# The S5 mixer of a hybrid decoder in chunks of four time steps, with its loads in another order

## The chip, the cores and the metric

The kernel runs on one core of a Trainium2 chip. The metric is device time in microseconds (us) of one execution, lower is better. Engines: TensorE (PE in the profile, its weight loads PEld), VectorE (DVE), ScalarE (ACT), GpSimd (POOL), and SyncE (SP), which here only issues DMAs.

## The reference, cut to what matters

Two decoder layers over 512 tokens of width 1024, in float32. Each has a mixer and then a mixture of 64 experts of which each token takes two. The change is in the mixer of layer 0. That mixer projects the normed tokens to 1536 columns: 512 for S5, 512 for the RG-LRU input, 512 for the RG-LRU gate.

```
def s5_mixer(u, ...):                       # u: 512 steps x 32 groups x 16 channels
    lb = exp((lam_re + i lam_im) dt)        # one complex decay per state, 64 states in a group
    bu[l] = Bbar u[l]                       # 16 channels -> 64 complex states, per group
    s[l]  = lb * s[l-1] + bu[l]             # over the 512 steps
    y = Re(C s) + D u
    y = gelu(y);  return y * sigmoid(y @ glu_w + glu_b)
def rglru_mixer(...): conv of width 4, two gates (sigmoid), h[l] = a[l] h[l-1] + b[l], times gelu(gate)
out = concat(ya, yb) @ w_out;  x = x + out
```

## The kernel before

Channels or states lie on the 128 partitions and time along the free axis. Two groups of 64 states fill the 128 partitions, so the 32 groups make NS5 = 16 blocks, each with a real and an imaginary part over T = 512 steps.

Four instruction streams run in order (even_tensor, even_vector, even_scalar, even_gpsimd) and meet by semaphores. SP's stream and POOL's hold the loads, in their order.

- Start: norm_sums, norm_rows, norm_tensor (32 transposes, L209) and the evacuations L186 (ACT) and L201 (DVE) make hT, the normed input with channels on partitions. even_tensor then projects in 12 blocks of 128 columns, 8 matmuls each (L309), evacuated by proj_out (ACT).
- Parameters: even_vector derives decays and Bbar in some sixty small operations, which go through the helpers tt, ts and stt (L484, L488, L490, L493): each waits for the one before.
- Tables: per block, phases (DVE) makes a phase for each of the 512 steps, table_scalar (ACT) four functions of it, tables (DVE) the cosine and sine. With these a complex decay becomes a rotation of the input, a real decay, and a rotation back.
- Scan: per block s, bu (PE, L345) makes the block's input from its 32 channels. products (DVE, L616 to L619) rotates it, L626 and L627 add, two scans of 512 steps (L636, L637) run with the real decay, GpSimd rotates back (L685 to L688), and PE contracts with C (L367: four matmuls of 32 output rows).
- RG-LRU: conv (L577, L579), gates (L332), exp/tanh/sqrt (L441 to L446), four scans (L600), ahead of the S5 scan on DVE.
- End: GELU (L454), GLU matmuls (L376), sigmoid (L457), product (L643), output projection in 8 tiles of 512 columns (out_lru L352 for the RG-LRU half, L387 for the S5 half), added to x (L406), and the norm of the next part.
- The experts: three slots of two experts each (ring buffers 0 to 3, wbuf, region_a) are filled by first_pair and moe_sync; slots 0 and 1 may be filled when the mixer has let go of their memory, slot 2 after the output projection. PE works through 32 pairs of experts (L1262, L1272, L1281, L1292).

A matmul in float32 shows as two MATMUL instructions in the profile, a transpose as one.

## Time and profile before

| | us |
|---|---|
| median of 3 runs (lowest, highest) | 1800.18 (1798.22, 1801.88) |
| the profiled execution's own time | 1798.09 |
| its span in the profile | 1796.2 |
| PE busy, of the span | 1405.1 (78%) |
| DVE busy | 577.4 (32%) |
| ACT busy | 305.9 (17%) |
| POOL busy | 384.0 (21%) |

The span holds, in order: the mixer of layer 0 (0 to 346 us), its experts (to about 900), the attention mixer of layer 1 (to about 1210) and its experts (to the end). Busy shares are means over all of these; the stage that is changed is the first, and the expert stages have the DMA engines full. A line given with a helper (L484) holds the work of many callers, told apart by shapes.

### The profile page before, as it was taken

What the parts mean: (1) busy time and instruction counts of PE and PEld (TensorE: products, weight loads), DVE (VectorE), ACT (ScalarE), POOL (GpSimd) and SP (SyncE); (2) the same over time, 40 slices, a digit from 0 to 9 for tenths busy, and PEclk for the clock granted to TensorE, in tenths of its full rate; (3) what the DMA queues carried; (4) which work ended last, traced back from release to release, by engine and by line L of the source; (5) the groups of instructions that cost most, each with busy time, mean ns of one, the idle gap of its engine ahead of it and who ended that gap; (6) DMA issues with size and microseconds to landing.
All of it is one profiled execution on the core that took longest, in us unless ns stands there. A gap on an engine that the chain in (4) does not pass through costs nothing.

```text
span 1796.2 us, 18735 instructions
## 1 busy us (share of the span) xinstructions
PE 1405.1 (78%) x5548; PEld 615.6 (34%) x5548; DVE 577.4 (32%) x1063; ACT 305.9 (17%) x594; POOL 384.0 (21%) x484
## 2 busy tenths in 40 slices
PE   5966879849878877777838969994897887887883
PEld 3421213523323323332325437544333322332331
DVE  5979991251111111111140665315111111111112
ACT  3671001101110001001023343211111001100100
POOL 2006881012322222222100000000222222222120
PEclk9986989969999999999968989996899989998997
DMA  7102003269999999999732020307699999999994
GB/s 215 47 8 86 1 0 152 95 253 391 390 403 403 406 400 399 407 411 389 309 105 100 0 106 1 153 35 281 255 396 400 395 402 398 402 412 396 393 366 179
DMA packets 81971, 464.27 MB, mean 258 GB/s; under 512 B 13504, under 2 KB 15584, under 8 KB 32384
## 3 DMA queue, kind: packets, MB, share of 16 engines
q1 hardware_dynamic: 68352, 435.81, 61.6%
q0 software_dynamic: 11840, 21.52, 3.8%
q10 hardware_dynamic: 1728, 6.29, 0.9%
q8 instruction: 29, 0.48, 0.1%
q14 instruction: 22, 0.18, 0.0%
HBM read 453.14 MB, written 18.94 MB: 263 GB/s over the span
## 4 chain that ended last, share of the span: by engine, by line
PE 37%; SPq 28%; DVE 18%; DMA 6%; issue 6%; ACT 3%; POOL 1%; POOLq 0%; DVEq 0%; ACTq 0%
SPq L1410 18%; PE ps L1272 12%; SPq L1415 10%; PE ps L1292 5%; DMA ring<-in_moe_w 3%; PE ps L398 3%; PE ps L1262 2%; PE ps L777 2%; DVE ring L637 2%; PE ps L387 2%; PE ps L209 1%; DMA region_a<-ytok 1%; PE ps L830 1%; DVE extra L484 1%; PE ps L352 1%
## 5 line engine op out<-in xcount | busy, mean ns | idle before, releaser
L1272 PE MATMUL ps<-ring,region_b 128*64 128x512 f32 x1408 | 347.7, 650 | 79.9 <-issue 53.1
L1376 DVE TENSOR_TENSOR extra<-extra,ps 128x256 f32<-128x256 f32 x64 | 27.0, 421 | 611.9 <-ACT extra L1328 611.9
L1272 PEld LDWEIGHTS ps<-ring,region_b 128*64 128x64 f32 x1408 | 116.9, 150 | 308.0 <-issue 269.8
L1272 PE MATMUL ps<-wbuf,region_b 128*64 128x512 f32 x320 | 159.5, 657 | 44.9 <-DMA region_a<-in_moe_w 28.0
L1292 PE MATMUL ps<-ring,extra 128*64 128x512 f32 x704 | 160.8, 598 | 34.8 <-DVE extra L1382 34.8
L1272 PE MATMUL ps<-region_a,region_b 128*64 128x512 f32 x320 | 159.7, 657 | 0.0
L1216 POOL DMA_INDIRECT region_b<-hrow,icol x128 | 118.6, 926 | 156.2 <-issue 156.2
L1228 POOL DMA_INDIRECT ytok<-extra,icol x128 | 112.2, 876 | 162.8 <-issue 162.8
L1328 ACT ACTIVATE extra<-ps 128x256 f32<-128x256 f32 x64 | 24.6, 384 | 589.0 <-PE ps L1272 589.0
L1389 DVE COPY extra<-ps 128x512 f32<-128x512 f32 x64 | 44.3, 692 | 248.0 <-PE ps L1292 248.0
L1226 POOL COPY icol<-blkidx 64x2 int32 (+1 forms) x64 | 11.2, 176 | 462.9 <-DVE extra L1389 462.9
L1272 PEld LDWEIGHTS ps<-wbuf,region_b 128*64 128x64 f32 x320 | 46.8, 151 | 152.1 <-issue 140.2
L1292 PEld LDWEIGHTS ps<-ring,extra 128*64 128x64 f32 x704 | 49.9, 136 | 115.4 <-issue 89.8
L1262 PE MATMUL ps<-con,region_b 128*128 128x128 f32 x512 | 75.7, 292 | 17.2 <-DMA region_b<-hrow,icol 17.2
L1262 PEld LDWEIGHTS ps<-con,region_b 128*128 128x128 f32 x512 | 63.2, 195 | 67.9 <-issue 67.9
L1292 PE MATMUL ps<-wbuf,extra 128*64 128x512 f32 x320 | 73.1, 597 | 16.7 <-DVE extra L1382 16.7
L1334 ACT ACTIVATE extra<-ps 128x512 f32<-128x512 f32 x64 | 38.2, 597 | 277.0 <-PE ps L1292 277.0
L309 PE MATMUL ps<-region_b,wbuf 128*128 128x512 f32 x192 | 83.1, 593 | 0.8 <-ACT region_b L186 0.8
L209 PE MATMUL ps<-con,region_a 128*128 128x128 f32 x128 | 24.1, 375 | 53.3 <-DVEq L161 35.6
L1214 POOL COPY icol<-blkidx 64x2 int32 (+1 forms) x64 | 13.6, 213 | 218.3 <-DVEq L1190 217.5
L1321 ACT ACTIVATE region_b<-ps 128x512 f32<-128x512 f32 x64 | 38.2, 597 | 93.9 <-PE ps L1262 93.9
L1371 DVE COPY region_b<-ps 128x512 f32<-128x512 f32 x64 | 44.3, 692 | 24.4 <-PE ps L1262 24.3
(288 smaller groups left out, 1746.6 us busy)
## 6 DMA issues: line engine op xcount, KB each, us to landing
ring<-in_moe_w SPq DMA_DIRECT2D x264, 1024.0 KB, 26.5
wbuf<-in_moe_w SPq DMA_DIRECT2D x80, 1024.0 KB, 26.4
region_a<-in_moe_w SPq DMA_DIRECT2D x40, 1024.0 KB, 28.7
region_a<-ytok SPq DMA_DIRECT2D x16, 512.0 KB, 4.6
wbuf<-in_ev_w_in SPq DMA_DIRECT2D x3, 2048.0 KB, 10.6
hrow<-region_a ACTq DMA_DIRECT2D x8, 512.0 KB, 15.3
wbuf<-in_mla_w_in SPq DMA_DIRECT2D x2, 1408.0 KB, 26.9
wbuf<-in_mla_w_uq SPq DMA_DIRECT2D x1, 2304.0 KB, 8.6
```

The lines of the kernel that those rows point to most:

```text
L209: last = TE.transpose(ps[:, 2 * c + k // 4, (k % 4) * P:(k % 4 + 1) * P], hs[:, k, :], ident)
L309: last = TE.matmul(ps[:, PB[n], :], w[:, k, (m % 4) * P:(m % 4 + 1) * P], hT[:, k, :], start=k == 0, stop=k == KC - 1)
L398: last = TE.matmul(ps[:, (n + 2) % 4, :], lhs(k, n // 2), wout[n % 2][:, k, :], start=k == 0, stop=k == KC - 1)
L1216: G.indirect_dma_start(xin[j][CAP * g:CAP * g + n, :], None, hrow[l], bass.IndirectOffsetOnAxis(ap=icol[0:n, 2 * j + g:2 * j + g + 1], axi ...
L1228: G.indirect_dma_start(ytok[l], bass.IndirectOffsetOnAxis(ap=icol[0:n, 4 + 2 * j + g:5 + 2 * j + g], axis=0), yo[j][CAP * g:CAP * g + n, : ...
L1262: last = TE.transpose(ps[:, k // 4, (k % 4) * PAIR:(k % 4 + 1) * PAIR], xin_block(j, k), ident)
L1272: last = TE.matmul(ps[CAP * g:CAP * (g + 1), 2 + j, :], xtr[j][:, k, CAP * g:CAP * (g + 1)], up_weights(2 * slot + g, k), start=k == 0, st ...
L1292: last = TE.matmul(ps[CAP * g:CAP * (g + 1), 6 + nh, :], hidT[j][:, f, CAP * g:CAP * (g + 1)], w2[2 * slot + g][:, f * D + nh * 512:f * D ...
L1371: V.tensor_copy(xtr[j][:, 0:4, :].rearrange("p k s -> p (k s)"), ps[:, 0, :])\
L1389: V.tensor_copy(yo[j][:, 0:512], ps[:, 6, :]).then_inc(ml["s_ye"][l], 1)
L1410: nc.sync.dma_start(w13[b][:, n, :], src).then_inc(s, 16)
L1415: nc.sync.dma_start(w2[b], src).then_inc(s, 16)
```

## The change

S5 works in chunks of LC = 4 steps, so NC = 128 chunks.

- The S5 projection is computed with time on the partitions (32 matmuls of 512 columns, one set for each step i within a chunk), evacuated by ACT to u4 and turned by 16 transposes to uT: for each block of 32 channels a tile of (4 steps x 32 channels) x 128 chunks.
- DVE makes the decay's powers 0 to 4 and with them bd, Bbar times the powers; 32 transposes and 8 evacuations make wb. GpSimd makes wc (C times the powers) and the decay tile dec.
- Input of a chunk: two matmuls of 128 columns for each block (32 in all) give it for all 128 chunks.
- Between chunks: one table of 16 x 128 phases, one rotation, and two scans over all 16 blocks side by side (2048 elements), with the fourth power of the decay; the first element of each block has decay zero.
- Within a chunk: a Toeplitz matrix of 128 x 128 for each block, made by 128 small matmuls (function toeplitz), evacuated by ACT (toep_out) and given D on its diagonal by GpSimd.
- Output: 64 matmuls with the Toeplitz tiles and 128 with the states before each chunk, all 128 rows deep, 32 output rows wide, 128 columns long, into four PSUM banks; GELU reads them there.
- The RG-LRU's vector part now stands behind the S5 scan. All of out_lru comes after the GLU matmuls.
- Loads: the identity ahead of x, the S5 columns of the input weights first; B and C as one transfer in place of six; both early expert slots when the S5 output and the RG-LRU are done, ahead of the barrier.
- The small parameter work up to the phase step moved ahead of the evacuations L186 and L201.

The removed code is in the functions printed above. Core of the diff:

```diff
 QK = NOPE + ROPE
...
+            TE.wait_ge(s_ev_x[0], 16)
+            hs = hT.rearrange("p k (c i) -> p k i c", i=LC)
+            for i in range(LC):
                 for k in range(KC):
-                    last = TE.matmul(ps[:, PB[n], :], w[:, k, (m % 4) * P:(m % 4 + 1) * P], hT[:, k, :],
+                    last = TE.matmul(ps[:, i, :], hs[:, k, i, :], wcol[0][:, k, :], start=k == 0, stop=k == KC - 1)
+                last.then_inc(s_s5p, 1)
...
+            TE.wait_ge(s_ev_x[1], 16)
+            project(wcol[1], 0, 4)
+            TE.wait_ge(s_s5e, U4E)
+            for q in range(MT):
+                for g in range(4):
+                    last = TE.transpose(ps[:, q, g * P:(g + 1) * P],
+                                        u4[:, 4 * q + g, :, :].rearrange("p i n -> p (i n)"), ident)
+                last.then_inc(s_s5p, 1)
+            for m in range(1, MT):
+                project(wcol[1], m, 4 + m)
...
+            for b in range(2):
+                for q in range(MT):
+                    if b:
+                        TE.wait_ge(s_s5e, U4E + q + 1)
+                    else:
+                        TE.wait_ge(s_pje, q + 1)
+                    for g in range(4):
+                        last = TE.transpose(ps[:, (4, 0)[b] + q, g * P:(g + 1) * P],
+                                            bd[b][:, 4 * q + g, :, :].rearrange("p i n -> p (i n)"), ident)
+                    last.then_inc(s_s5p, 1)
+
+            TE.wait_ge(s_s5e, WBE)
+            for hf in range(2):
+                for g in range(8):
+                    s = 8 * hf + g
+                    for b in range(2):
+                        last = TE.matmul(ps[:, (4, 0)[hf] + 2 * b + g // 4, (g % 4) * P:(g % 4 + 1) * P],
+                                         wb[b][:, s * P:(s + 1) * P], uT[:, s, :], start=True, stop=True)
+                last.then_inc(s_s5p, 1)
...
+            def toeplitz(q, bank):
+                for g in range(4):
+                    s = 4 * q + g
+                    for b in range(2):
+                        for i in range(LC):
+                            last = TE.matmul(ps[32 * i:32 * i + 32, bank, g * P + 32 * i:(g + 1) * P], b0[b][:, s, :],
+                                             wc[b][:, s, 0:LC - i, :].rearrange("p j n -> p (j n)"),
+                                             start=g == 0 and b == 0, stop=g == 3 and b == 1)
+                last.then_inc(s_s5p, 1)
+
+            TE.wait_ge(s_wc, 2)
+            TE.wait_ge(s_pre, 1)
+            toeplitz(0, 6)
+            toeplitz(1, 7)
...
+            TE.wait_ge(s_ev_x[2], 16)
+            TE.wait_ge(s_pre, 2)
+            project(wcol[0], 0, 0)
+            project(wcol[0], 1, 1)
+            TE.wait_ge(s_gts, 2 * MT)
+            toeplitz(2, 4)
+            toeplitz(3, 5)
+            project(wcol[0], 2, 2)
+            project(wcol[0], 3, 3)
...
+            TE.wait_ge(s_wc, 5)
+            for q in range(MT):
+                for j in range(LC):
+                    for g in range(4):
+                        r = slice(32 * g, 32 * g + 32)
+                        TE.matmul(ps[r, 4 + q, j * NC:(j + 1) * NC], toep[:, 4 * q + g, 32 * j:32 * j + 32],
+                                  uT[:, 4 * q + g, :], start=j == 0, stop=False)
+            for q in range(MT):
+                TE.wait_ge(s_st, q // 2 + 1)
+                for j in range(LC):
+                    for b, st in enumerate((pa, pc)):
+                        for g in range(4):
+                            r = slice(32 * g, 32 * g + 32)
+                            s = 4 * q + g
+                            last = TE.matmul(ps[r, 4 + q, j * NC:(j + 1) * NC], wc[b][:, s, j + 1, :],
+                                             st[:, s * NC:(s + 1) * NC], start=False,
+                                             stop=j == LC - 1 and b == 1)
                 last.then_inc(s_cy, 1)
...
+            TE.wait_ge(s_yb, MT)
+            TE.wait_ge(s_wb[0], 16)
+            TE.wait_ge(s_wb[1], 16)
+            for n in range(4):
+                out_lru(n)
...
+            lru_out(1)
+            S.wait_ge(s_ph, 1)
+            S.activation(tabs, ph, ACT.Sin, scale=math.pi).then_inc(s_sn, 1)
+            alink(S.activation(tk, ph, ACT.Abs))
+            S.activation(tk, tk, ACT.Sin, scale=-math.pi, bias=halfpi).then_inc(s_sn, 1)
+            S.wait_ge(s_sn, 1)
+            S.activation(tabc, tabs, ACT.Square).then_inc(s_sn, 1)
+            lru_out(2)
+            lru_out(3)
+            for n in range(2 * MT):
+                S.wait_ge(s_s5p, UTE + n + 1)
+                S.activation(wb[n // MT][:, (n % MT) * T:(n % MT + 1) * T], ps[:, ((4, 0)[n // MT] + n % MT), :],
+                             ACT.Copy).then_inc(s_s5e, 1)
+
+            S.wait_ge(s_wc, 3)
...
+            for dst, (p1, p2, op) in ((bd[0], (pwr, pwi, ALU.subtract)), (bd[1], (pwi, pwr, ALU.add))):
+                for i in range(LC):
+                    V.tensor_tensor(bt4[0][:, :, i, :], qr, up(p1, LC - 1 - i), ALU.mult)
+                    ins = V.tensor_tensor(bt4[1][:, :, i, :], qi_, up(p2, LC - 1 - i), ALU.mult)
+                vlink(ins)
                 for g in range(2):
                     r = slice(64 * g, 64 * g + 64)
-                    tt(dst[r, :, 16 * g:16 * g + 16], btmp[r, :, :], btmp2[r, :, :], op)
+                    tt(dst[r, :, :, 16 * g:16 * g + 16], bt4[0][r, :, :, :], bt4[1][r, :, :, :], op)
             V.nop().then_inc(s_brd, 1)
...
+            tt(by_group(ph), tcb, rho_hi[:, :, None].to_broadcast([P, NS5, NC]), ALU.mult)
+            ts(tk, ph, ROUND, ALU.add)
+            ts(tk, tk, -ROUND, ALU.add)
+            tt(ph, ph, tk, ALU.subtract)
+            tt(by_group(tk), tcb, rho_lo[:, :, None].to_broadcast([P, NS5, NC]), ALU.mult)
+            tt(ph, ph, tk, ALU.add)
+            V.nop().then_inc(s_ph, 1)
...
+            for hf in range(2):
+                cols = slice(hf * HC, (hf + 1) * HC)
+                bank = (4, 0)[hf]
+                V.wait_ge(s_s5p, XH + hf + 1)
+                ur = ps[:, bank:bank + 2, :].rearrange("p b n -> p (b n)")
+                ui = ps[:, bank + 2:bank + 4, :].rearrange("p b n -> p (b n)")
+                V.tensor_tensor(pa[:, cols], ur, tabc[:, cols], ALU.mult)
+                V.tensor_tensor(pb[:, cols], ui, tabs[:, cols], ALU.mult)
+                V.tensor_tensor(pc[:, cols], ui, tabc[:, cols], ALU.mult)
+                vlink(V.tensor_tensor(pd[:, cols], ur, tabs[:, cols], ALU.mult))
+                V.nop().then_inc(s_pre, 1)
+            V.tensor_tensor(pa, pa, pb, ALU.add)
+            tt(pc, pc, pd, ALU.subtract)
+            V.wait_ge(s_wc, 4)
+            V.tensor_tensor_scan(pb, dec, pa, 0.0, ALU.mult, ALU.add)
+            vlink(V.tensor_tensor_scan(pd, dec, pc, 0.0, ALU.mult, ALU.add))
+            V.memset(by_group(pa)[:, :, 0:1], 0.0)
...
+                cols = slice(hf * HC, (hf + 1) * HC)
...
+                vlink(V.tensor_tensor(part(pc, 1, NC), part(pb, 0, NC - 1), part(tabs, 0, NC - 1), ALU.mult))
+                vlink(V.tensor_tensor(pb[:, cols], pd[:, cols], tabs[:, cols], ALU.mult))
+                vlink(V.tensor_tensor(pd[:, cols], pd[:, cols], tabc[:, cols], ALU.mult))
+                V.tensor_tensor(part(pa, 1, NC), part(pa, 1, NC), part(pb, 0, NC - 1), ALU.subtract)
+                V.tensor_tensor(part(pc, 1, NC), part(pc, 1, NC), part(pd, 0, NC - 1), ALU.add).then_inc(s_st, 1)
 
...
+            G.wait_ge(s_prm, 2)
+            pwr, pwi = pw
...
+            G.tensor_tensor(t1, co(cre), up(pwr), ALU.mult)
+            glink(G.tensor_tensor(t2, co(cim), up(pwi), ALU.mult))
+            for g in range(2):
+                r = slice(64 * g, 64 * g + 64)
+                glink(G.tensor_tensor(wc[0][r, :, :, 16 * g:16 * g + 16], t1[r, :, :, :], t2[r, :, :, :], ALU.subtract))
+            glink(G.tensor_scalar(cre, cre, -1.0, None, ALU.mult))
+            G.tensor_tensor(t1, co(cre), up(pwi), ALU.mult)
+            glink(G.tensor_tensor(t2, co(cim), up(pwr), ALU.mult))
+            for g in range(2):
+                r = slice(64 * g, 64 * g + 64)
+                glink(G.tensor_tensor(wc[1][r, :, :, 16 * g:16 * g + 16], t1[r, :, :, :], t2[r, :, :, :], ALU.subtract))
+            G.nop().then_inc(s_wc, 1)
+            G.wait_ge(s_brd, 1)
+            G.tensor_copy(b0[0], bd[0][:, :, LC - 1, :])
+            glink(G.tensor_copy(b0[1], bd[1][:, :, LC - 1, :]))
...
+            sp.dma_start(con[:, 0:P], a["p_const"][:, 0:P]).then_inc(s_id, 16)
...
+            sp.dma_start(wcol[0], wv[:, :, 0:512]).then_inc(s_ev_x[0], 16)
+            sp.dma_start(con[:, P:C_END], a["p_const"][:, P:C_END]).then_inc(s_con, 16)
+            sp.dma_start(wcol[1], wv[:, :, 512:1024]).then_inc(s_ev_x[1], 16)
+            sp.wait_ge(s_s5p, LC)
             sp.dma_start(wcol[0], wv[:, :, 1024:1536]).then_inc(s_ev_x[2], 16)
...
+            sp.wait_ge(s_pj, 2 * MT)
+            sp.dma_start(glu, a["p_glu_w"]).then_inc(s_gw, 16)
+            sp.dma_start(wout0[1], wo[:, :, 512:1024]).then_inc(s_wb[1], 16)
+            sp.wait_ge(s_st, 1)
+            sp.dma_start(wout0[0], wo[:, :, 0:512]).then_inc(s_wb[0], 16)
+            sp.wait_ge(s_cy, MT)
+            sp.wait_ge(s_yb, MT)
             first_pair(0, 0)
-            sp.wait_ge(s_bar, 4)
             first_pair(0, 1)
```

## Rows read from the trace of the kernel before

**Rows 1.** Windows: each engine's busy us (xinstructions), granted PE clock, DMA share, GB/s.
```profile
380.00:400.00 20.00, 11.13 (x46) 5.76 (x48) 5.79 (x18) 1.88 (x2) 6.04 (x9) 0.55 0.39 156
400.00:420.00 20.00, 18.48 (x94) 7.39 (x92) 3.58 (x7) 2.56 (x5) 3.96 (x6) 1.00 0.81 331
440.00:460.00 20.00, 18.35 (x93) 8.01 (x91) 3.70 (x8) 2.69 (x6) 5.92 (x8) 1.00 1.02 384
860.00:880.00 20.00, 16.17 (x74) 6.58 (x70) 3.37 (x7) 2.56 (x5) 1.94 (x3) 0.91 0.91 353
```

**Rows 2.** Chain of waits in order of time: start, us, what.
```profile
294.11 6.87 PE ps L352 x16
342.21 0.70 DVE x L406
```

**Rows 3.** DVE in order of time, scan of S5: start, us, engine line operation tiles.
```profile
221.91 1.75 DVE L627 TENSOR_TENSOR ring<-ring 128x512 f32<-128x512 f32 x1
223.58 0.68 DVE L616 TENSOR_TENSOR extra<-ps,ring 128x512 f32<-128x512 f32 x1
225.97 1.21 DVE L636 TENSOR_TENSOR_SCAN ring<-smalls,ring 128x512 f32<-128x512 f32 x1
227.10 2.22 DVE L637 TENSOR_TENSOR_SCAN ring<-smalls,ring 128x512 f32<-128x512 f32 x1
229.83 1.75 DVE L627 TENSOR_TENSOR extra<-extra 128x512 f32<-128x512 f32 x1
```

**Rows 4.** POOL over the same stretch.
```profile
221.48 1.62 POOL L685 TENSOR_TENSOR region_a<-ring 128x512 f32<-128x512 f32 x1 [1.16 <-DVE ring L637]
223.07 1.72 POOL L686 TENSOR_TENSOR region_a<-ring 128x512 f32<-128x512 f32 x1
224.75 1.26 POOL L687 TENSOR_TENSOR region_a<-ring 128x512 f32<-128x512 f32 x1
225.98 2.26 POOL L688 TENSOR_TENSOR region_a<-ring 128x512 f32<-128x512 f32 x1
```

**Rows 5.** PE in order of time: start of the projections; GLU; last expert matmuls of a pair.
```profile
24.61 20.84 PE L309 MATMUL ps<-region_b,wbuf 128*128 128x512 f32 x48 [0.83 <-ACT region_b L186]
...
103.52 7.76 PE L332 MATMUL ps<-extra,region_a 64*64 64x512 f32 x24 [14.13 <-ACT ring L435]
...
280.11 14.00 PE L376 MATMUL ps<-region_a,extra 128*128 128x512 f32 x32 [2.28 <-ACT region_a L454]
...
408.30 7.04 PE L1272 MATMUL ps<-ring,region_b 128*64 128x512 f32 x32
```

**Rows 6.** PE in attention, tiles of 128 columns, in order of time.
```profile
1081.00 0.39 PE L828 MATMUL ps<-ring 128*128 128x128 f32 x2
1081.23 0.39 PE L829 MATMUL ps<-con 128*128 128x128 f32 x2
1081.54 0.48 PE L830 MATMUL ps<-ring 64*128 64x128 f32 x2
```

**Rows 7.** Groups of instructions, 0 to 330 us: shapes xcount, busy us, mean ns.
```profile
L209 PE MATMUL ps<-con,region_a 128*128 128x128 f32 x32 | 6.1, 376 | 17.7 <-DMA con<-in_p_const 17.7
L484 DVE TENSOR_TENSOR extra<-extra,smalls 128x256 f32<-128x256 f32 x4 | 1.7, 424 | 0.1
```

**Rows 8.** DVE and ACT in order of time: small operations, table load, Sin.
```profile
8.29 1.04 ACT L178 ACTIVATE extra<-x 128x1024 f32<-128x1024 f32 x1
36.51 1.65 DVE L484 TENSOR_TENSOR smalls<-smalls 128x16 f32<-128x16 f32 x8
122.47 1.28 ACT L465 ACT_TABLE_LOAD   x1
123.77 0.63 ACT L465 ACTIVATE region_a<-region_a 128x512 f32<-128x512 f32 x1
```

**Rows 9.** Windows of 2 us around an idle stretch of PE, columns as in rows 1.
```profile
92.00:94.00 2.00, 0.00 (x0) 0.00 (x0) 1.90 (x4) 0.39 (x1) 0.00 (x0) 1.00 0.00 0
94.00:96.00 2.00, 0.00 (x0) 0.00 (x0) 1.77 (x5) 1.94 (x4) 0.00 (x0) 0.57 0.00 0
```

More of the change, by code:

```diff
@@ L20 @@
 NS5 = 16
+LC = 4
+NC = T // LC
 H = 8
@@ L241, in hybrid_decoder @@
+        iT = r1[:, 2048:4096].rearrange("p (m t) -> p m t", m=MT)
+        gT = regb[:, 0:2048].rearrange("p (m t) -> p m t", m=MT)
+        glu = regb[:, 2048:4096].rearrange("p (k n) -> p k n", k=MT)
+        yg = pb.rearrange("p (m t) -> p m t", m=MT)
+        ya = pd.rearrange("p (m t) -> p m t", m=MT)
         s5p = small(16 * 3)
         lam_re, lam_im, ldt = s5p[:, 0:16], s5p[:, 16:32], s5p[:, 32:48]
-        s5q = [small(16) for _ in range(14)]
+        s5q = [small(16) for _ in range(15)]
@@ L244, in hybrid_decoder @@
+        pw = [small(16 * (LC + 1)).rearrange("p (s j) -> p s j", s=NS5) for _ in range(2)]
+        dskip = small(16)
+        eye32 = small(32)
         chp = small(MT * 10)
@@ L355, in even_tensor @@
-            bu(0)
-            bu(1)
-            bu(2)
-            TE.wait_ge(s_pje, 12)
-            for s in range(NS5):
-                if s + 3 < NS5:
-                    bu(s + 3)
-                TE.wait_ge(s_st, s + 1)
-                if s % 4 == 0 and s >= 8:
-                    TE.wait_ge(s_yd, s // 4 - 1)
-                r = slice(32 * (s % 4), 32 * (s % 4) + 32)
-                for j, (cm, g) in enumerate(zip((0, 2, 1, 1), prod[s % 2])):
-                    last = TE.matmul(ps[r, (s // 4) % 2, :], cmat[:, cm, s, :], g, start=j == 0, stop=j == 3)
+                    TE.matmul(ps[:, 4 + (n + 2) % 4, :], gT[:, k, (n // 2) * P:(n // 2 + 1) * P],
+                              wout0[n % 2][:, MT + k, :], start=k == 0, stop=False)
@@ L386, in even_tensor @@
                 for k in range(MT):
-                    last = TE.matmul(ps[:, (n + 2) % 4, :], uT[:, k, (n // 2) * P:(n // 2 + 1) * P],
-                                     wout[n % 2][:, k, :], start=False, stop=k == MT - 1)
+                    last = TE.matmul(ps[:, 4 + (n + 2) % 4, :], ya[:, k, (n // 2) * P:(n // 2 + 1) * P],
+                                     wout0[n % 2][:, k, :], start=False, stop=k == MT - 1)
                 last.then_inc(s_op, 1)
@@ L430, in even_scalar @@
-            proj_out(6)
-            proj_out(7)
+            S.activation(l1, l1, ACT.Ln, bias=1.0).then_inc(s_pra, 1)
+            for i in range(LC):
+                S.wait_ge(s_s5p, i + 1)
+                S.activation(u4[:, :, i, :], ps[:, i, :].rearrange("p (s n) -> p s n", s=NS5), ACT.Copy)\
+                    .then_inc(s_s5e, 1)
+            lru_out(0)
+            for q in range(MT):
+                S.wait_ge(s_s5p, U4E + q + 1)
+                S.activation(uT[:, 4 * q:4 * q + 4, :].rearrange("p s c -> p (s c)"), ps[:, q, :], ACT.Copy)\
+                    .then_inc(s_s5e, 1)
@@ L432, in even_scalar @@
+            S.wait_ge(s_wc, 3)
+            toep_out(0, 6)
+            toep_out(1, 7)
             for m in range(MT):
@@ L483, in tt, with lru_out @@
+        def lru_out(m):
+            S.wait_ge(s_pj, m + 1)
+            if m == 0:
+                S.wait_ge(s_xpad, 1)
+            S.activation(xT[:, m, 3:3 + T], ps[:, 4 + m, :], ACT.Copy).then_inc(s_pje, 1)
         def tt(o, p, q, op):
```

438 lines of the change are left out of this document (178 added, 260 removed).

## The prediction

> **What bounds the kernel now.** I read the windows first, to see which stages can carry a gain onward. From 400 to 880 us the DMA engines are full (share 0.81 to 1.02, 331 to 384 GB/s), and from 380 to 400 us they are at 0.39 [rows 1]: by then the three expert slots are full, and loading goes on when PE lets go of the first. So the experts of layer 0 end a fixed time after their first pair starts. That start hangs on the mixer's end by the same norm and routing in both kernels. Earlier expert loads gain nothing: the slots were full before PE used them.
>
> Next the chain of waits in order of time: the output projection ends when DVE adds its last tile at 342.2 us [rows 2]. Everything behind moves with this mark. Hence: new time = 1798.1 (the profiled execution's own time) minus the shift of 342.2. That execution lies 2.1 below the median of the runs, so I add 2.1.
>
> Then DVE and POOL in the scan, which the chain crosses from 142 to 268 us: DVE is never idle, a block takes 7.9 us (L627 starts at 221.91 and at 229.83), and 16 of them make 127 us [rows 3]. The same L627 that takes 1.75 us holds 0.6 us of work: it starts at 221.91 beside L685 and ends just after L685 lets go; L637 has 2.22 against L636's 1.21, while L616, which reads PSUM, keeps 0.6 to the next [rows 3, 4]. After the scan come 74 us with PE full: GLU 14.0, 8 matmuls of out_lru 6.9, the rest 41.2 (300.97 to 342.2) [rows 2, 5].
>
> **The change part by part.** DVE's scan work falls sharply: products 8 of 1024 elements from PSUM (1.2 each, twice 0.6) 9.6; two sums of 2048 at 2.2 (four times 0.6, less the starts), 4.4; two scans of 2048 (four times 1.13) 9.1; rotating back 12 of 1024 at 1.2, 14.4; sum 38 us for 127. The rotation leaves GpSimd. But PE's list grows, and I expect the end of the path to be PE's. Its prices:
>
> - A matmul of 512 columns is 8 of 48 instructions' worth: 20.84 us / 48 = 0.43 an instruction, 0.86 each [rows 5]. The 32 for S5, 32 for the RG-LRU input, 32 for the gate cost 27.5 us each, as before.
> - A transpose 0.19 (6.1 / 32) [rows 7]: 16 make 3.0, 32 make 6.1.
> - A matmul 128 deep, 128 wide, 128 columns: 1081.00 to 1081.23 for two instructions, 0.11 each [rows 6]. The 64 instructions of the chunk inputs cost 7.2.
> - The small ones, 32 rows wide: toeplitz 256 instructions (32 to 128 columns), Toeplitz output 128, state output 256; 640 in all. No row shows this shape. The nearest are 0.11 for a full-width tile, and the expert matmuls, whose two halves of 64 rows run side by side: 32 instructions of 512 columns in 6.9 us, 0.215, half of 0.43 [rows 5]. Four side by side would be 0.027, none side by side 0.11 (toeplitz 0.067, at its mean of 80 columns). I take 0.06, the half that the rows show: toeplitz 7.7 for each half, outputs 7.7 and 15.4. Ends: 21 us less, 20 us more.
>
> Now the path, in us from the start. **Start.** Transposes no longer wait until 17.7 for all constants. But both evacuations now stand behind the parameter work: DVE's norm rows end at 15.9, 18 small operations of 0.21 and four copies of 0.7 end near 23; ACT has a table load more. PE starts at 24 (24.6 before). It was idle for 6 us by then, and PE's clock fell to 0.57 in the window behind an idle one [rows 9]; some 4 us at half speed cost 2: 26. Between 23 and 28 is open.
>
> **To the tables.** S5 27.5, RG-LRU block 0 6.9, 16 transposes 3.0, blocks 1 to 3 20.6: PE is free at 84. Before it can go on it needs lru_out(2) and (3), which stand in ACT's queue behind the four table functions, and these wait for the phases from DVE. DVE: 25 small operations of 0.21 (1.65 / 8) [rows 8] to 28.2, which releases GpSimd's wc. From then on both run operations with two SBUF inputs. Before, each waited for the whole operation of the other in turn [rows 3, 4]. GpSimd's are 1280 long: 2.5 times 1.26 = 3.1 each, eight of them and a short one, 25 us [rows 4]; in that time DVE gets through about nine of its small ones instead of all. Then 3 small ones, six of 256 (0.42) [rows 7] 2.6, 16 of 256 and four of 1024 elements 11.5: bd at 71. Phases (four of 2048 at 2.2, two at 1.2) and waits 14: 85. ACT: table load 1.3, four functions of 2048 at 2.0 to 2.3 [rows 8]: 94.6, lru_out(2) and (3) to 95.8. If the two engines did not stop each other, phases would be ready at about 60, hidden behind PE's 84, and 9 us go away; if GpSimd's took 2.26 for 512 elements, as the blocked L688 did, it is 20 more. I take the 9, by the unblocked row.
>
> The Trainium skill (SBUF — State Buffer, "Who interferes with whom") says of the pair of ports that the two engines share that it is an exclusive lock, held for a whole instruction. The trace agrees at 512 elements; no row has a 3 us operation against a 0.2 us one. By a plain sharing of bandwidth the 9 would be about 3.
>
> **To the S5 output.** Last transposes and evacuations: 100. Chunk inputs 7.2: 107.3. toeplitz needs PSUM that DVE empties: DVE has made the tables (98.2) and two convs (104.5), products of the first half to 109.3. toeplitz(0), (1): 117. Gates 8 (24 instructions took 7.76, half of it at the low clock) [rows 5]: 125. Gate projection 13.7, toeplitz 7.7, projection 13.7: 160.1. Outputs 7.7 and 15.4: 183.2. What must be there by then is: the states on DVE end at 109.3 + 4.8 + 4.4 + 9.1 + 14.4 = 142, and GpSimd's diagonal at about 155. **To the end.** GELU 0.7, GLU 14.0, out_lru 13.7 (6.9 before: two of its tiles lost their cover, the scan), the rest 41.2: 252.8. The RG-LRU vector part, behind the scan on DVE and behind toep_out(3) on ACT, ends near 164, 34 us before out_lru asks for it. DMA: the 12 MB for the slots go out at 184 and take 30 us at 400 GB/s, under PE's work; the output weights go before them.
>
> Shift 342.2 − 252.8 = 89.4. Time 1798.1 − 89.4 + 2.1 = 1711.
>
> **Rivals.** *Side by side.* The small matmuls run four at a time, 21 less, or the table stall is covered, 9 less: 1690, or 1681 with both. For it: two at a time halve the time exactly [rows 5]. Against it: an instruction every 0.03 us is nowhere in the trace. The Trainium skill (TensorE: Matmul & The Clock Gate, "Part 3: Packing small matmuls — row/col tiling") gives 2.38 times for three column tiles of 32 at 512 columns and a floor near 25 ns for any start to start. As an estimate from that page, some 0.045 an instruction, ten us off my sum: 1701. No row here has three tiles or more.
>
> *One after the other.* The 32-wide matmuls of 128 columns do not overlap, 20 more: 1731. With GpSimd's operations at the blocked price as well, 11 beyond my 9, 1742. For it: the change from L829 to L830 costs 0.16 an instruction instead of 0.11 [rows 6], so tile changes may cost. Also PE's short idle stretches could hold it at the low clock through the small ones.
>
> *Tile changes drain the array.* Every small matmul runs as if alone. A lone 128-column instruction shows 0.39 / 0.48 us for two overlapped, some 0.28 for one. 640 of these are 179 us instead of 38: 141 more, 1852, slower by 52. It decides from 0.20 each on ((89.4 + 38.4) / 640). Against it: the expert matmuls change their column half at every instruction without loss [rows 5].
>
> *The path does not move.* If the mixer were not what the experts wait for, the time would stay at 1800. Against it: the DMA engines idle at 380 to 400 us for want of a free slot [rows 1], so the experts wait for PE, and PE for the mixer.
>
> **Chances.** Forecast 0.48, side by side 0.25, one after the other 0.24, drained 0.02, no move 0.01. Time 1711. The range takes in both ends of the two unknown prices: 1681 to 1742. About 0.2% (3.6 us) can be told from no change: faster 0.97, same 0.01, slower 0.02.
>
> **What will show it.** Right: in the profile after, the last addition of the output projection near 253 us and the expert stage as long as before; L636's successors near 4.5 us each; PE busy without gaps from 109 to 253 us. The state output's 256 instructions in about 15 us settle the small matmuls (7 or 27 for the rivals). The wait of ACT's first table function for DVE, ending near 85, and DVE's small operations of 0.2 us stretched to 3 us while GpSimd makes wc, show the stall. Wrong: the states coming after 160 us, so that DVE and not PE sets the end; evacuations held at the start by the parameters' transfer beyond 28; an expert stage that is longer than before by more than 3 us.

## The result, and the profile of the changed kernel

| | us |
|---|---|
| before, median (lowest, highest) | 1799.68 (1798.22, 1801.88) |
| after, median (lowest, highest) | 1690.34 (1690.18, 1692.09) |
| ratio, 95% interval | 0.9398 [0.9384, 0.9412] |
| after, the profiled execution's own time, its span | 1692.09, 1689.8 |

The change takes 109.3 us off. The forecast was 1711, 20.7 too high. The chain of waits in order of time (start, us, what) gives the mark that answers to [rows 2]: the last addition of the output projection starts at 232.1 us instead of 342.2, 110.1 earlier. PE and issue gaps ("issue": PE waits for nothing that the profile shows) are the chain's only pieces from 105.9 us to this mark, so PE sets the end. From 15.4 to 98.1 us, where toeplitz begins, the chain runs through DVE and, for the tables, ACT: norm, parameters, bd, phases, tables, convolutions, products. Of DVE's work only what follows the first products is off the path.

```profile
73.54 2.30 DVE region_a L541
75.92 1.91 ACT ring L481
...
83.51 0.51 DVE ring L677
...
84.65 2.30 DVE ring L678
...
143.19 3.63 PE ps L399 x128
146.82 3.04 PE ps L408 x107
149.85 1.74 issue
151.59 3.70 PE ps L408 x128
155.29 3.06 issue
158.34 0.85 PE ps L408 x21
159.19 1.21 issue
160.41 16.70 PE ps L417 x32
177.10 13.73 PE ps L391 x32
190.84 13.73 PE ps L431 x32
...
232.07 0.70 DVE x L450
```

PE in order of time, for [rows 5]. In brackets stands the wait before a group, with what ended it. L357 and L399 are the small matmuls that had no row before.

```profile
23.07 29.14 PE L311 MATMUL ps<-wbuf,region_b 128*128 128x512 f32 x64 [5.17 <-DVE region_b L203]
...
81.27 1.04 PE L339 MATMUL ps<-con,extra 128*128 128x128 f32 x8
84.01 2.89 PE L339 MATMUL ps<-con,extra 128*128 128x128 f32 x24 [1.71 <-ACT ring L538]
88.39 7.41 PE L348 MATMUL ps<-ring 128*128 128x128 f32 x64 [1.49 <-ACT ring L490]
98.10 3.65 PE L357 MATMUL ps<-ring,gain 128*32 128x128 f32 x128 [2.30 <-DVEq L693]
101.68 1.93 PE L375 MATMUL ps<-ring 64*64 64x512 f32 x8
105.89 5.82 PE L375 MATMUL ps<-ring 64*64 64x512 f32 x24 [2.27 <-ACT ring L499]
```

The 128 instructions of L357 take 3.65 us: 0.028 each, where the sum had 0.06. PE waits 1.7 and 1.5 us around 84 us, where the sum had 9 more.

DVE and POOL while wc is made, for [rows 3, 4, 8]:

```profile
25.86 1.74 DVE L541 TENSOR_TENSOR smalls<-smalls 128x16 f32<-128x16 f32 x8
27.95 4.79 DVE L541 TENSOR_TENSOR smalls<-smalls 128x16 f32<-128x16 f32 x3
33.06 6.65 DVE L541 TENSOR_TENSOR smalls<-smalls 128x16 f32<-128x16 f32 x8
```
```profile
27.81 2.36 POOL L750 TENSOR_TENSOR ring<-ring,smalls 128x1280 f32<-128x1280 f32 x1 [12.49 <-DVEq L609]
...
32.57 5.97 POOL L754 TENSOR_TENSOR ring<-ring 64x1280 f32<-64x1280 f32 x2
```

Eight operations of 16 columns take 1.74 us before 27.6 and eight others of the same shape 6.65 beside POOL: two of these spread to 2.5 and 2.8, about the length of one of POOL's.

The two scans that stand for the 32 before (two in each block of [rows 3]):

```profile
107.33 4.42 DVE L697 TENSOR_TENSOR_SCAN extra<-wbuf,extra 128x2048 f32<-128x2048 f32 x1
111.67 4.40 DVE L698 TENSOR_TENSOR_SCAN region_a<-wbuf,region_a 128x2048 f32<-128x2048 f32 x1
```

And windows over the start of the experts and over their stage, columns as in [rows 1]: DMA is again full behind the first pair, and idle just before it, with PE at 0.53 of its clock.

```profile
270.00:290.00 20.00, 11.27 (x44) 5.86 (x46) 5.89 (x18) 1.88 (x2) 6.05 (x9) 0.53 0.04 11
290.00:770.00 480.00, 394.03 (x1764) 153.99 (x1760) 65.50 (x123) 48.31 (x92) 117.48 (x177) 0.94 1.00 394
```

The first expert matmul moves from 393.07 to 283.07 us, by 110.0, the last of layer 0 by 107.1, the span by 106.4. The profiled execution is the slowest of its four, 1.8 above their median, where the one before lay 2.1 below its own. Between the two profiled executions the time fell by 106.0, and 4.1 of the mark's 110.1 were lost behind it, 2.9 of them in the experts of layer 0. So it is in part luck that the medians differ by so nearly the shift of the mark.

### The profile page after: what moved, and what is told of

Read it like the earlier page. It is cut to its first block, busy times and chain, and to the rows that moved or that the text cites. A ratio compares the mean times of both kernels' runs of the same rounds, so it can differ in the third digit from the quotient of the medians.

```text
span 1689.8 us, 19504 instructions
## 1 busy us (share of the span) xinstructions
PE 1341.6 (79%) x6100; PEld 630.5 (37%) x6100; DVE 480.5 (28%) x904; ACT 287.4 (17%) x562; POOL 321.6 (19%) x439
## 4 chain that ended last, share of the span: by engine, by line
PE 41%; SPq 30%; DVE 12%; issue 7%; DMA 6%; ACT 3%; POOLq 0%; POOL 0%; DVEq 0%; ACTq 0%
SPq L1506 20%; PE ps L1368 13%; SPq L1511 10%; PE ps L1388 6%; DMA ring<-in_moe_w 4%; PE ps L442 3%; PE ps L873 2%; PE ps L316 2%; PE ps L431 2%; PE ps L391 2%; DVE ring L541 1%; DMA region_a<-ytok 1%; PE ps L926 1%; DVE extra L541 1%; PE ps L1358 1%
## 5 line engine op out<-in xcount | busy, mean ns | idle before, releaser
L1368 PE MATMUL ps<-wbuf,region_b 128*64 128x512 f32 x320 | 168.4, 687 | 45.1 <-DMA region_a<-in_moe_w 24.6
L1368 PE MATMUL ps<-region_a,region_b 128*64 128x512 f32 x320 | 168.5, 688 | 0.0
L1388 PE MATMUL ps<-wbuf,extra 128*64 128x512 f32 x320 | 73.1, 597 | 16.7 <-DVE extra L1478 16.0
L316 PE MATMUL ps<-region_b,wbuf 128*128 128x512 f32 x128 | 55.8, 594 | 0.0
```

What stands on the lines that cost most here:

```text
L316: last = TE.matmul(ps[:, bank, :], w[:, k, m * P:(m + 1) * P], hT[:, k, :], start=k == 0, stop=k == KC - 1)
L1368: last = TE.matmul(ps[CAP * g:CAP * (g + 1), 2 + j, :], xtr[j][:, k, CAP * g:CAP * (g + 1)], up_weights(2 * slot + g, k), start=k == 0, st ...
L1388: last = TE.matmul(ps[CAP * g:CAP * (g + 1), 6 + nh, :], hidT[j][:, f, CAP * g:CAP * (g + 1)], w2[2 * slot + g][:, f * D + nh * 512:f * D ...
```

## The experiments

In all of them "mark" is the start of the last addition (232.1 us in the changed kernel), read from the chain of one execution, while the time is the median of all. The executions with the marks took 1680.7 us in the early-weights kernel and 1678.9 in the mixed one, 4.7 and 3.5 below their medians; in the others they lie within 2 us of it.

**One column group at a time.** What made the small matmuls cheap: their size, or the way round the four column groups?

```
 L357  for g: for b: for i (column group)   ->  for i (column group): for g: for b
 L399  for j: for g (column group)          ->  for g (column group): for j
 L408  for j: for b: for g (column group)   ->  for g (column group): for j: for b
```

> The changed kernel with the loops of the 640 small matmuls reordered, same instructions and sums: consecutive ones now stay in one group of 32 columns of the array instead of going round the four. Changed kernel: 1690.3 us, end of the output projection 232.1 us, toeplitz 3.65 to 3.68 us per 128 instructions (0.028 each), state output 7.6 us of work. Theory (four column groups run side by side): an instruction of 128 columns costs 0.11 again, the 384 output instructions 31 us more, the 256 of toeplitz (80 columns in the mean, 0.067) 10 more; time 1725 to 1735, mark 265 to 275. Rival (a tile 32 columns wide is simply cheap, about 0.03, in whatever order): 1690, mark 232.

Measured: 1707.88 us, ratio 0.9483 [0.9467, 0.9499], mark 252.2. PE in order of time; then the state output in its chain:

```profile
99.07 8.76 PE L357 MATMUL ps<-ring,gain 128*32 128x128 f32 x128 [3.40 <-DVEq L693]
...
131.48 7.22 PE L357 MATMUL ps<-ring,gain 128*32 128x128 f32 x128
...
152.56 7.73 PE L399 MATMUL ps<-ring 128*32 128x128 f32 x125
```
```profile
160.62 21.44 PE ps L408 x253
182.06 1.20 issue
```

Order alone costs 17.5 us of time and 20.1 of the mark, so the groups do run side by side; the rival falls. (The mark also holds a first toeplitz half partly at the low clock, 8.8 for 7.2 us, and against that a GLU 2.7 faster.) But the price is smaller than expected, and the time with it, 1725 to 1735 forecast: 0.062 (L399) and 0.084 (L408) an instruction, not 0.11. In L399 eight instructions in a row stay in one group, in L408 sixteen. Eight cost 0.50 us, sixteen 1.344: eight more cost 0.844, or 0.1055 each, which is the serial price. Measured by that price, a run of either length is short by some 3.3 instructions. The issue gaps of L408 are gone at this slower pace, though DMA is as full as before (share 1.05 from 160 to 166 us, 0.90 still from 168 to 169).

**Runs of four.** The last reading, tested.

```
 L399  for j: for g       ->  for h in 0,1: for g: for j in 2h, 2h+1
 L408  for j: for b: for g ->  for j: for g: for b
```

> The changed kernel with the two output stages (384 small instructions) reordered so that four instructions in a row stay in one group of 32 columns (two in the changed kernel; 8 and 16 in the group-major kernel, which cost 0.0625 and 0.084 each). Theory (each group works off its own instructions at 0.107 apiece, and PE gets some 3.3 instructions ahead of a busy group before it is held: 8 - 0.5/0.107 = 3.3, 16 - 1.344/0.107 = 3.4): runs of four cost nothing, Toeplitz output 3.6 to 4.0 us per 128 instructions, state output 7.2 to 8.5 us of work, mark 232, time 1690. Rival 1 (the price rises steadily with the length of the run, 0.028, some 0.045, 0.0625, 0.084): 6 to 7 us more, mark 238, time 1697. Rival 2 (no look-ahead, only exact alternation overlaps): 0.06 or more each, 12 us more.

Measured: 1689.59 us, ratio 0.9387 [0.9372, 0.9401], mark 232.5. The Toeplitz output:

```profile
146.82 3.77 PE L398 MATMUL ps<-ring 128*32 128x128 f32 x128
```

Runs of four cost nothing: 0.029 an instruction there, 7.8 us of work for the 256 of the state output (0.0305). Both rivals fall. The price of a run is thus the larger of its share of four groups side by side and of its serial length less some three instructions. That a queue of about three instructions for each group is behind it is an inference from four run lengths (two, four, eight and sixteen).

What these runs do not separate is the price at the bottom: a quarter of 0.11 is 0.028, but toeplitz, with 80 columns in the mean, costs 0.028 as well and not a quarter of 0.067. One of its four groups has 128 columns in every round and may set the pace; or an instruction may cost 0.028 at the least, whatever its columns. No run tests it.

**No wc on GpSimd.** The nine operations that make wc are left out, so wc is zero.

```
-  G.tensor_tensor(t1, co(cre), up(pwr), ...)   # and the other eight, L750 to L760
```

> The changed kernel without the nine GpSimd operations that build wc (left out of the computation; wc stays zero). Theory (each engine waits for the other's whole operation, but nearly all of it lies beside PE): DVE's small operations take 0.2 us again instead of about 2.5, bd is done at 42 to 46 us instead of 62.4, the phases at 55 to 60 instead of 75.8, and of that only the 1.5 to 3.2 us that PE waited around 84 and 90 us reach the mark: 229 to 231, time 1687 to 1690. Rival 1 (the prediction's 9 us of stall on the path): mark 223, time 1681. Rival 2 (plain sharing of bandwidth): bd no more than 8 us earlier.

Measured: 1683.99 us, ratio 0.9349 [0.9331, 0.9368], mark 228.4. DVE in order of time:

```profile
27.83 0.60 DVE L541 TENSOR_TENSOR smalls<-smalls 128x16 f32<-128x16 f32 x3
...
28.75 1.65 DVE L541 TENSOR_TENSOR smalls<-smalls 128x16 f32<-128x16 f32 x8
...
54.94 2.29 DVE L541 TENSOR_TENSOR region_a<-region_a 128x2048 f32<-128x2048 f32 x1
```

The three and the eight operations take 0.60 and 1.65 us for 4.79 and 6.65; bd is done at 43.8 instead of 62.4 us, the phases at 57.2 instead of 75.8. So the two engines do stop each other for whole operations, for 18.6 us: more than the sharing rival allows and twice what the forecast put on the path. Yet toeplitz starts at 95.67 instead of 98.10: 2.4 us reach the path, or 3.3 if one counts from the end of PE's projections, which came 0.9 later in this run (82.14 for 81.27). Another 1.3 of the mark is the GLU's clock (15.4 us for 16.7). The time fell by 6.3, 2.6 more than the mark; since its output differs, so may the routing of its experts, and I do not read that rest.

**Output weights late, and early.** Are the gaps in L408 PE's own, or do the full DMA engines make them?

```
 changed kernel          late (e3)              early (e4)
 wait projections 8      wait state output      wait first states (123 us)
 load glu, half 1        load glu, half 1,      load half 0
 wait first states       half 0                 wait projections 8: load glu
 load half 0                                    wait state output: load half 1
```

> The changed kernel with glu and both halves of the output weights issued only after the state output (L408), so that the DMA engines are quiet in it. Changed kernel: L408 146.8 to 159.2 with 4.8 us of issue gaps around 7.6 us of work, GLU 16.7 us at a clock near 0.5 in its first 6 us, mark 232.1. Theory (the full DMA engines hold up PE's supply of instructions): L408 takes 7.6 to 8.5 us and ends near 155; glu lands some 5 us later, so the GLU still starts near 160 and the mark is 230 to 233. Rival (the gaps are PE's own, from what these instructions are): L408 takes 12.4 as before, the GLU starts at 164, mark 235 to 237, time 1694.

> The changed kernel with the first half of the output weights issued when the first states are done (123 us), glu at 143 as before, the second half only after the state output. DMA is quiet from about 147 to 155 us. Theory (full DMA engines hold up PE's instructions): no gaps in L408, it ends near 155, the GLU starts near 156 with PE's clock still full and takes 14.0 instead of 16.7, mark 224 to 226, time 1682 to 1684. Rival 1 (gaps are PE's own): mark 232, time 1690. Rival 2 (gaps follow the load wherever it is): 1 to 3 us of gaps appear in the toeplitz and gate projection at 125 to 130 us instead, mark 226 to 229.

Measured: late 1690.87 us, ratio 0.9391 [0.9378, 0.9404], mark 234.6; early 1685.47 us, ratio 0.9359 [0.9346, 0.9373], mark 226.7. The chain of the late one:

```profile
150.17 7.03 PE ps L408 x256
157.21 6.87 DMA region_b<-in_p_glu_w
164.13 15.51 PE ps L417 x32
```

and of the early one:

```profile
149.39 7.13 PE ps L408 x256
156.52 1.21 issue
157.74 13.97 PE ps L417 x32
```

(L417 is the GLU.) In both the gaps are gone, 256 instructions in 7.0 to 7.1 us. Windows of both kernels, the changed one first, show what differs beside them: the last columns are PE's clock, DMA share and GB/s.

```profile
150.00:154.00 4.00, 2.41 (x88) 2.41 (x92) 2.85 (x3) 1.16 (x1) 2.66 (x2) 1.00 1.05 396
154.00:158.00 4.00, 1.29 (x48) 1.02 (x40) 0.00 (x0) 1.13 (x1) 0.82 (x2) 1.00 1.05 387
```
```profile
149.00:153.00 4.00, 4.00 (x154) 3.98 (x148) 3.93 (x4) 1.18 (x1) 2.84 (x2) 1.00 0.25 102
153.00:157.00 4.00, 3.52 (x129) 3.25 (x118) 1.46 (x1) 2.77 (x3) 2.24 (x3) 1.00 0.01 4
```

With the DMA engines full PE gets as few as 48 matmuls in 4 us, with them quiet 154 in 4. The gaps do not fall anywhere: in each of the six kernels with the loads as in the changed one and the fast order in L408, they stand behind its 107th and its 235th matmul, 128 apart, or 256 instructions with the weight loads. The DMA queue named "instruction" moves one packet of 0.02 MB for each such stretch. In the changed kernel two such packets fall into these windows of 0.1 us (packets, MB, share), 149.10:149.20 and 155.80:155.90:

```profile
q8 instruction: 1, 0.02, 60.4%
q8 instruction: 1, 0.02, 68.8%
```

The gaps end at 151.59 and 158.34, each 2.5 us later; in the kernel without wc they stand at 146.8 and 153.4, and the gaps end 2.5 and 2.6 us later. In the early kernel they stand between 149.5 and 150.0 and between 153.0 and 153.5, and there is no gap. Counted from the start of L408 that is 0.1 to 0.6 and 3.6 to 4.1 us, against 2.3 and 9.0 in the changed kernel. So PE waits for its instructions, and their packets come late when the DMA engines are full. Pace counts too: the group-major kernel works through 12 matmuls an us instead of 35, its packets come at 160 and 168 us beside full DMA engines, and it has no gap. A full DMA alone does not do it either: toeplitz 2 of the early kernel ran from 128.0 to 131.5 us at full pace beside a DMA share of 1.01 and kept its 3.7 us; the nearest packets are at 122.5 and 132.0. With that rival 2 of the early kernel falls, and rival 1 (mark 232) by its mark.

The late kernel's gain is eaten by the wait for glu, 6.9 us, not the 5 expected, and its mark, 234.6, lies 1.6 beyond what was given. Both lose 1.7 us in the first toeplitz half (5.3 us for 3.65, in the early one at a clock of 0.55), and the late one another 1.4 in the gates behind it. That puts the early one's mark 0.7 beyond what was given. Its time, 1.5 beyond as the median of five from 1680.7 to 1686.0, cannot be put down to it: the execution with this trace is the fastest.

**The gate projection between the gates.** On top of the early output weights:

```
 for m in 0..3:
     gates of block m
+    if m < 2: project block m of the RG-LRU gate
```

> The kernel of the early output weights (mark 226.7, time 1685.5) with the first two blocks of the gate projection (3.43 us each) put between the RG-LRU gates of blocks 0, 1 and 2. There the gates take 10 us, 2.3 of it PE waiting for ACT's sigmoid. Theory: the waits are covered, nothing else moves: mark 224 to 225, time 1682 to 1684. Rival 1 (the chunk inputs' second half is not consumed yet when the first projection wants its bank): up to 1 us of it lost, 225.5. Rival 2 (the later gates delay the RG-LRU's vector part past 172 us, when out_lru asks for it): mark later than 227.

Measured: 1682.39 us, ratio 0.9353 [0.9341, 0.9366], mark 224.6. Gates and both blocks take 21.7 us (103.46 to 125.17) where they took 10.0 and 13.9, 2.2 less; 0.7 of it goes to a new wait for ACT before toeplitz 2. From the start of toeplitz to the mark it is 126.5 us instead of 127.6, so the edit is worth 1.1; the other us of the mark was there before it. The theory's numbers hold, half for another reason. At 8.0 us below the changed kernel (of the two medians) no version of the study is faster; its interval overlaps that of the early kernel, so the edit's own gain is told by the trace and not by the time.

**The start.** The load order undone in the changed kernel; and the changed order alone in the kernel before.

```
 e7:  x, constants whole, weights      (transposes wait for all constants)
 e8:  identity, x, constants, weights  (kernel before, DVE waits for constants after its evacuations)
```

> The changed kernel with the order of loads at the start undone: the constants in one piece behind x, and the transposes wait for all of them. Changed kernel: transposes from 10.98 us, S5 projection from 23.07. Theory (PE's start hangs on the identity, as before, where transposes began at 17.7 and the first matmul stood at 24.6): start at 24.5 to 26, mark 233.5 to 235, time 1692 to 1693.5. Rival (the start hangs on the evacuations behind DVE's parameter work alone): start at 23.1, no change.

> The kernel before with the changed start alone: identity loaded first, then x, then the other constants; DVE waits for them after its evacuations. Before: transposes from 17.7 us, first matmul 24.61. Theory (start edit alone is worth a few us where no parameter work stands ahead of the evacuations): first matmul at 19 to 21.5, time 3 to 5 us less than before, 1795 to 1797, so 3 to 5 % of the whole change's 109 could have come from it. Rival (the first matmul then waits for the weights or the parameters, which land no earlier): within 1.5 us of before.

Measured: e7 1688.52 us (five runs from 1687.9 to 1697.5), ratio 0.9402 [0.9382, 0.9422], mark 233.4; e8 1797.52 us, ratio 0.9993 [0.9984, 1.0002]. PE in order of time of e7, then of e8:

```profile
16.00 5.26 PE L211 MATMUL ps<-con,region_a 128*128 128x128 f32 x32 [16.00 <-DMA con<-in_p_const]
22.09 27.83 PE L311 MATMUL ps<-wbuf,region_b 128*128 128x512 f32 x64 [0.83 <-DVE region_b L203]
...
86.62 4.88 PE L339 MATMUL ps<-con,extra 128*128 128x128 f32 x24 [6.61 <-ACT ring L538]
```
```profile
19.11 1.97 PE L209 MATMUL ps<-con,region_a 128*128 128x128 f32 x8 [3.42 <-DVE region_a L195]
23.08 27.24 PE L309 MATMUL ps<-region_b,wbuf 128*128 128x512 f32 x56 [2.00 <-DMA wbuf<-in_ev_w_in]
```

Both theories fall. Undoing the reorder makes PE start a us earlier: the last part of x is there at 12.5 instead of 13.7 us, so DVE is through its norm rows and the 18 small operations ahead of its evacuations 1.2 us earlier (19.25 for 20.48). And PE starts at full clock, after a wait of 0.8 us instead of 5.2, since its transposes end just before. But ACT's evacuations now end at 21.9 us instead of 18.7 and hold up ACT's part of the parameter work, so DVE's part behind it is 2.6 us later (its first operation beside wc starts at 30.5 instead of 27.95), and PE pays for it with 6.6 us at the last transposes instead of 1.7; toeplitz starts 2.9 later. The theory's mark is nearly met by this other way. In e8 the last part of x arrives at 16.1 us (its chain), and then the weights are late, as its rival had it. The changed load order alone is worth about 2 of the 109 us: 1.9 in e8, with an interval from 2.9 to no change.

**The scans twice; the second expert pair after the mixer.**

```
 e9:   for _ in range(2): scan pb; scan pd
 e10:  first_pair(0, 0); wait for the mixer's end; first_pair(0, 1)
```

> The changed kernel with both scans of 2048 elements run twice (4.42 and 4.40 us more on DVE; the same values). Theory (from the toeplitz stage on PE sets the end; the first states are done at 123.3 us and asked for at 146.8, the last RG-LRU scan ends at 152.9 and is asked for at 176.9): DVE's marks 8.8 us later, no change of the time, mark 232 within 1, 1688 to 1692. Rival (DVE's work still counts in the path through a buffer or through the wait between scans and the other engines): 2 to 9 us more.

> The changed kernel with the wait before the second expert pair's loads put back (they start after the mixer, at about 240 us instead of 166). Theory (the loads of the second pair are hidden twice over, by PE's output projection or by the norm, routing and first pair, 50 us until 283): no change, 1689 to 1692. Rival (a later start of the 12 MB pushes the whole DMA-bound stage of layer 0, from 283 to 787 us): 4 to 15 us more.

Measured: e9 1691.7 us, ratio 0.9402 [0.9381, 0.9422]; e10 1689.03 us, ratio 0.9384 [0.9363, 0.9404]. In e9 the four RG-LRU scans start at 152.5 to 160.1 us instead of 143.2 to 150.7, and the time stays. Its mark is 234.5, outside the 1 us given: 2.0 of it is there at the start of L399 (145.12 for 143.12), 1.7 of them from a toeplitz half that took 5.3 us, ahead of anything a scan could delay. In e10 the first expert matmul is at 284.7, behind a mark of 233.6. DVE is off the path from the scans on, and the early load of the second pair is worth nothing that these runs can tell.

**Two attempts at the stall at 84 us.** On top of the mixed version: e11 moves one of ACT's two evacuations ahead of the tables and one between them, and DVE's third convolution ahead of the tables' last products; e12 besides starts GpSimd's spreading of the decay at 92 us.

```
 e11 ACT:  lru_out(2); Sin; Abs; Sin; lru_out(3); Square     (was: Sin; Abs; Sin; Square; lru_out(2), (3))
 e12 POOL: wait chunk inputs (was: wait projections 4); copy dec; clear dec
```

> The kernel with early output weights and mixed gates (mark 224.6, time 1682.4), and besides: ACT evacuates RG-LRU block 2 before the phases' tables and block 3 between them, and DVE's third convolution runs before the tables' last two products. There PE waits 1.4 us at the last transposes for those evacuations and 2.3 at toeplitz for DVE, and its clock is at half behind that. Theory: the first wait goes, the second shrinks by 1 to 2 us, products start near 91 us; mark 221 to 223, time 1679 to 1681. Rival (the phases, ready only at 75.8 because DVE and GpSimd stop each other, keep the tables and so the products where they are): mark 224, time 1682.

> The kernel just before this one, and besides GpSimd's two operations that spread the decay (2.0 and 1.1 us, begun near 82.5) start only with the chunk inputs at about 92 us. With them at 82.5 a product of DVE's tables waits 0.65 to 1.75 us in the changed kernel and its variants. Theory (the engines stop each other for whole operations): 0.6 to 1.7 us off the products' start if the operation then falls beside DVE's products, which read PSUM; mark 1 lower than the kernel just before, time 1 lower. Rival (it only stops another of DVE's operations then): equal within 0.5.

Measured: e11 1683.11 us, ratio 0.9354 [0.9336, 0.9372], mark 223.8; e12 1682.4 us, ratio 0.9346 [0.9327, 0.9364], mark 225.2. PE in e11:

```profile
81.77 3.93 PE L339 MATMUL ps<-con,extra 128*128 128x128 f32 x32
89.00 8.87 PE L348 MATMUL ps<-ring 128*128 128x128 f32 x64 [3.29 <-ACT ring L490]
99.22 3.65 PE L357 MATMUL ps<-ring,gain 128*32 128x128 f32 x128 [1.35 <-DVEq L693]
```

The first wait is gone as meant, and the second is now 3.3 us, since ACT's evacuations of the transposes still stand behind the tables; after it the chunk inputs run 1.5 us longer. The rival holds for e11: ready phases set this stretch. e12 gives nothing measurable either (its mark is 1.4 later than e11's); its theory of a us is not shown.

## Why the prediction was right or wrong, by its own steps

Right were the frame and the mechanism: the bound (the experts wait for PE, PE for the mixer), the fall of DVE's scan off the path, PE as the new end, the last 55 us (out_lru and rest 54.9 forecast, 55.0 measured), the expert stage unchanged within 3 us, and a shift of the mark that came through to the time (110.1 and 109.3). Of its own tests, DVE's products of 1.2 us, scans of 4.4 and the stretched small operations came as said; "PE busy without gaps from 109 us" did not.

Wrong were two sizes, both towards too slow, and smaller things, three of which gave a part back. In us, of the mark:

| step of the forecast | forecast | measured | difference |
|---|---|---|---|
| PE free after RG-LRU block 3 | 84 | 81.3 | -2.7 |
| from there to the chunk inputs ("I take the 9") | 16 | 7.1 | -8.9 |
| to toeplitz | 9.3 | 9.7 | +0.4 |
| toeplitz, both halves, at 0.06 ("I take 0.06") | 15.4 | 7.2 | -8.2 |
| gates | 8 | 10.0 | +2.0 |
| two gate projections | 27.4 | 27.9 | +0.5 |
| Toeplitz output at 0.06 | 7.7 | 3.7 | -4.0 |
| state output at 0.06 | 15.4 | 12.4 | -3.0 |
| GELU and issue | 0.7 | 1.2 | +0.5 |
| GLU | 14.0 | 16.7 | +2.7 |
| to the end | 54.9 | 55.0 | +0.1 |
| mark | 252.8 | 232.1 | -20.7 |

*The price of a small matmul* is the larger miss, 15.2 us. The prediction named the 0.027 of four side by side and took 0.06, the half that two column halves show in [rows 5]. That row speaks for more: 0.215 for 0.43 is a perfect half, so groups that share nothing, and then four quarters give 0.11 / 4 = 0.028, the number measured for 128 columns (whether it is a quarter or a least price stays open). Without the issue gaps the miss is 20.0. The group-major kernel shows that the overlap comes from the order, which the diff already showed: the innermost loop goes round the groups.

The Trainium skill (TensorE: Matmul & The Clock Gate, "Part 3: Packing small matmuls — row/col tiling") has 2.38 times for three column tiles, from which the prediction estimated 0.045. Here four column tiles gave 0.1055 / 0.028, about 3.8. The floor near 25 ns for start to start stands on the same page under "Wait — 56ns, not 53.3ns?"; the 28 measured lie just above it. The measurement decides.

*The stall of DVE and GpSimd* was right as a mechanism and too large as a term of the path. The sum had ACT's four functions end at 94.6 us; they ended at 83.5. Of the 11.1 us, 9.2 are the phases, ready at 75.8 and not 85, and 2.0 ACT's functions themselves, 7.6 us and not 9.6. The phases were early because bd came at 62.4 and not 71: GpSimd's nine operations took 22.7 us, not 25, and DVE got through sixteen of its own beside them, twelve small ones and four of 256 columns, where the sum had nine. The sum was also wrong in itself: its terms as given, 28.2 + 25 + 0.6 + 2.6 + 11.5, make 67.9 and not 71. Without wc the phases come at 57.2, so the stall is 18.6 us long, of which 2.4 to 3.3 reach the path. The rest lies beside PE's projections; the forecast had this cover, but ended the stall too late for it.

The Trainium skill (SBUF — State Buffer, "Who interferes with whom") calls the pair of ports an exclusive lock held for a whole instruction. The traces agree: operations that take 0.2 us without wc take 2.3 to 2.8 beside GpSimd's of 2.4 to 3.0.

*The start* gave 2.7 more: PE began at 23.1 and not 24, lost 1.5 and not 2 to the low clock, and from block 0 to the last transposes took 29.2 us and not 30.5, since the 16 transposes cost 0.11 each and not 0.19.

*What took some back.* Gates: the 32 instructions took 7.8 us, as the sum had it, but PE waited another 2.3 for ACT's sigmoid, which it left out; in the row that it used, half of the 7.8 was at the low clock [rows 5]. Issue gaps of 4.8 us in the state output: without them the term would have been 7.6. The early-weights kernel and the packets of the queue "instruction" show them to come with the output weights' load. The GLU, 2.7: its first 6 us ran at half clock (0.50 to 0.53 from 160 to 166 us). It took 14.0 us in six of the variants and 15.4 to 16.7 in the others. PE had stood idle before all the slow ones, for the late kernel's (15.5) in the wait for glu; but runs of four had gaps as well, 4.0 us in all, and took 14.0. What drops the clock there is not settled.

So 1690 is the rival *side by side*, though not by either of its two sums: with both its gains, 1681, plus what came back, 4.8 + 2.7 + 2.0. (The start and the smaller rows of the table nearly cancel against the side-by-side price, 0.028 for 0.027.) The range held it. The rivals *one after the other*, *drained* and *no move* are out.

## What to carry to other kernels

Where a shape has no row, ask what two known shapes say of the resource: if halves overlap perfectly, price quarters at a quarter and put the half at the far end of the range, and read the loop order, since it decides whether they overlap at all. A stall between two engines is a term of the path only from the point where its cover ends, so its end has to be worked out as closely as its length. Here bd was forecast 8.6 us too late, 3.1 of them by an error of addition, and that was nearly all of the second miss. After a gain on PE, look at what is loaded beside its fastest instructions: here moving two loads of 2 MB out of it was worth 4.9 of the 8.0 us that the mixed version gains.

## What the runs showed of the hardware that was not expected

- Up to four instructions in a row in one group of 32 columns cost nothing if the next ones go to others (0.028 to 0.0305 us each); eight cost 0.062 and sixteen 0.084.
- Full DMA engines (share 1.05) opened gaps of 1.7 and 3.1 us in a sequence of 35 small matmuls in a us, and none in one of 12 in a us. The gaps stand 128 matmuls apart, at the same two places in every kernel that has them, and in the changed kernel and the one without wc each ends 2.5 to 2.6 us behind a packet of the DMA queue "instruction".
- The same code and the same wait of 2.3 us before it ended once at full clock (3.65 us for the first half of toeplitz) and once at the low one (5.32); after waits of 2.6 to 3.4 us in six other runs it took 5.3 us or more (one of them in the group-major order), after 1.4 in four runs 3.65.
- A weight load of 128 columns whose elements lie 16 bytes apart took 308 ns (L311), 190 for adjacent ones (L391); under a matmul of 512 columns it does not show.
